# A hybrid decoder block on one core: attention heads spliced into the weight stream at other places, unnormalised differential weights, and the gate's modulation rows moved and given to VectorE alone

## The reference

```python
shift, scale, gate = split(c @ w_ada + b_ada, 3)
h = rms_norm(x, g_pre) * (1 + scale) + shift
proj = h @ w_in            # MLA q / kv latent / rope key, diff q / k / v, two SiLU gates, two merge gates
o_mla  = mla_attention(...)                  # 8 heads, softmax, causal
lam = exp(sum(lq1 * lk1)) - exp(sum(lq2 * lk2)) + lambda_init
a = p[:, 0] - lam * p[:, 1]                  # 8 differential heads, each with two softmax maps
o_diff = rms_norm(a @ v, g_subln) * (1 - lambda_init)
y_mla, y_diff = (o_mla * silu(gate_mla)) @ w_o_mla, (o_diff * silu(gate_diff)) @ w_o_diff
merged = sigmoid(mg_mla) * y_mla + sigmoid(mg_diff) * y_diff
x = x + gate * rms_norm(merged @ w_out, g_post)
```

## Time and profile before

| what | value |
|---|---|
| median of 3 runs | 806.49 us (806.04 to 807.21) |
| profiled execution, its own time | 807.88 us |
| its span | 806.1 us |
| PE busy | 763.9 us (95%) |
| DVE busy | 560.5 us (70%) |
| ACT busy | 399.4 us (50%) |
| POOL busy | 129.4 us (16%) |
| DMA | 190.23 MB, mean 236 GB/s |
| TensorE's granted clock, mean | 0.992 |

### The profile page before, as it was taken

One profiled execution on the slowest core, in us unless ns is written; L12 is line 12 of the kernel. 1 busy time (PEld: TensorE's weight loads), 2 busy tenths in 40 slices (PEclk: granted clock), 3 DMA queues, 4 the chain that ended last, 5 costly groups with the idle time before them and its releaser, 6 DMA issues.

```text
span 806.1 us, 9875 instructions
## 1 busy us (share of the span) xinstructions
PE 763.9 (95%) x3565; PEld 624.8 (77%) x3565; DVE 560.5 (70%) x795; ACT 399.4 (50%) x634; POOL 129.4 (16%) x149
## 2 busy tenths in 40 slices
PE   4789999999999999999999999989999999989995
PEld 4567888787888788888887777767888888868884
DVE  4888888798676845455546999888777766475553
ACT  4466646445665565444446464635344443343441
POOL 2000000000000000000004441454264254210000
PEclk9899999999999999999999999999999999999998
DMA  9999999999664465555456767666687778765542
GB/s 340 392 321 378 342 312 332 322 332 309 213 202 133 156 210 158 157 157 152 136 178 233 244 211 231 194 228 207 210 288 264 234 259 274 276 231 183 189 151 104
DMA packets 116795, 190.23 MB, mean 236 GB/s; under 512 B 9797, under 2 KB 42762, under 8 KB 116234
## 3 DMA queue, kind: packets, MB, share of 16 engines
q1 hardware_dynamic: 116624, 189.56, 71.5%
q10 hardware_dynamic: 122, 0.04, 0.0%
HBM read 187.47 MB, written 2.10 MB: 235 GB/s over the span
## 4 chain that ended last, share of the span: by engine, by line
PE 69%; DVE 14%; DMA 5%; issue 5%; ACT 4%; SPq 2%; POOL 1%; DVEq 0%; POOLq 0%; ACTq 0%
PE ps L1581 21%; PE ps L1585 21%; PE ps L1582 21%; DVE w_both L1328 5%; DVE ada_acc L1125 3%; DMA w_raw<-in_w_out 2%; DMA w_raw<-in_w_in 2%; SPq L416 1%; ACT w_both L884 1%; DMA ada_ring<-in_w_ada 1%; PE ps L1373 1%; PE ps L1417 1%; PE ps L1426 1%; PE ps L1430 1%; PE ps L1456 1%
## 5 line engine op out<-in xcount | busy, mean ns | idle before, releaser
L1328 DVE TENSOR_TENSOR w_both<-w_raw,w_both 128x1024 fp32r<-128x1024 f32 x248 | 303.6, 1233 | 149.6 <-ACT w_both L884 148.6
L884 ACT CAST w_both<-w_raw 128x1024 fp32r<-128x1024 f32 x248 | 258.8, 1051 | 283.7 <-PE ps L1585 204.9
L1581 PE MATMUL ps<-w_both,h_hi 128*128 128x512 f32 x704 | 284.4, 404 | 6.7 <-DVE w_both L1328 6.1
L1585 PE MATMUL ps<-w_both,h_lo 128*128 128x512 f32 x704 | 275.7, 392 | 0.3 <-DVE h_lo L1237 0.3
L1582 PE MATMUL ps<-w_both,h_hi 128*128 128x512 f32 x704 | 274.9, 390 | 0.0
L1581 PEld LDWEIGHTS ps<-w_both,h_hi 128*128 128x128 f32 x704 | 132.6, 188 | 40.3 <-issue 10.3
L1585 PEld LDWEIGHTS ps<-w_both,h_lo 128*128 128x128 f32 x704 | 132.4, 188 | 29.9 <-DVE h_lo L1237 1.0
L1582 PEld LDWEIGHTS ps<-w_both,h_hi 128*128 128x128 f32 x704 | 132.8, 189 | 26.3 <-issue 0.7
L1125 DVE SCALAR_TENSOR_TENSOR ada_acc<-ada_ring,cols,ada_acc 128x512 f32<-128x512 f32 x112 | 78.1, 743 | 1.7 <-DMA ada_ring<-in_w_ada 1.7
L534 POOL TENSOR_SCALAR gate_ring<-gate_ring,cols 128x512 f32<-128x512 f32 x28 | 50.0, 1787 | 65.9 <-DMA gate_ring<-in_w_ada 65.3
L1581 PE MATMUL ps<-w_both,o_hi 128*128 128x512 f32 x128 | 50.7, 396 | 0.0
(11 more groups left out here) (224 smaller groups left out, 728.0 us busy)
## 6 DMA issues: line engine op xcount, KB each, us to landing
w_raw<-in_w_in SPq DMA_DIRECT2D x177, 512.0 KB, 4.7
ada_ring<-in_w_ada SPq DMA_DIRECT2D x128, 256.0 KB, 6.5
gate_ring<-in_w_ada SPq DMA_DIRECT2D x32, 512.0 KB, 5.1
w_raw<-in_w_out SPq DMA_DIRECT2D x32, 512.0 KB, 3.7
w_raw<-in_w_o_mla SPq DMA_DIRECT2D x16, 512.0 KB, 4.4
w_raw<-in_w_o_diff SPq DMA_DIRECT2D x16, 512.0 KB, 5.7
w_raw<-in_w_ukv SPq DMA_DIRECT2D x8, 512.0 KB, 4.0
x_tok<-in_x SPq DMA_DIRECT2D x2, 1024.0 KB, 6.0
```

The source lines that it names most:

```text
L884: act.copy(w_hi[:, p % RING, :], w_raw[:, p % RING, :]).then_inc(hi_done, 1)
L1328: dve.tensor_tensor(w_lo[:, p % RING, :], w_raw[:, p % RING, :], w_hi[:, p % RING, :].bitcast(F32), ALU.subtract).then_inc(lo_done, 1)
L1581: mm(o, lhsT=s_hi[:, k, q], rhs=hi, start=first and r == 0, stop=False)
L1585: ins = mm(o, lhsT=s_lo[:, k, q], rhs=hi, start=False, stop=last and r == tiles - 1)
```

## The change

- Weights of a differential head: before, both maps were scaled with their own inverse sums and subtracted. Now the second map is multiplied by `ratio` = -lam * sum1 / sum2 and added to the first, which stays unnormalised. The missing factor 1 / sum1 (`first_scale`) is applied where the squares are made and, by one more GpSimd instruction, to the inverse root.
- `dve_o_lo` takes one instruction where it took two or three.
- Places: differential heads have t = s+5, v = s+7, g = s+10, MLA heads +4, +6, +8, so that TensorE's work for three neighbouring heads meets behind one piece, and there are two insertions per head. Before, there were three. `diff_weights` stands at s+7, `diff_out` still at v+5, which is now the same piece, behind the next head's weights.
- Gate: VectorE adds odd and even rows, GpSimd none. Part k stands at piece 173 + 2k (to 235); `gate_sum` is at 187, 204, 220, 236. `bias_gain` lies elsewhere and its first load waits for the differential heads.

The diff, without the declarations:

```diff
@@ -247,7 +249,7 @@
         ada_rings = [sb("ada_ring", [P, ADA_RING // 2, 2, 2, 2 * P], F32, r_c),
                      sb("ada_ring2", [P, ADA_RING // 2, 2, 2, 2 * P], F32, r_b)]
         silu_gate = sb("silu_gate", [P, 2, TOK, D // 2], F32, r_c)
-        bias_gain = sb("bias_gain", [P, 2, CH], F32, r_c + 4 * KB)
+        bias_gain = sb("bias_gain", [P, 2, CH], F32, r_c + 8 * KB)
         m_hi = sb("m_hi", [P, KT, SEQ], F32R, r_b)
         m_lo = sb("m_lo", [P, KT, SEQ], F32R, r_b + 16 * KB)
@@ -367,8 +368,8 @@
         MLA0 = last_piece("ukv", 0) + 6
         DIFF0 = first_piece("mm", 0) + 4
-        mla_at = [(MLA0 + 4 * h, MLA0 + 4 * h + 3, MLA0 + 4 * h + 5, MLA0 + 4 * h + 7) for h in range(HEADS)]
-        diff_at = [(DIFF0 + 5 * h, DIFF0 + 5 * h + 6, DIFF0 + 5 * h + 8, DIFF0 + 5 * h + 11) for h in range(HEADS)]
+        mla_at = [(MLA0 + 4 * h, MLA0 + 4 * h + 4, MLA0 + 4 * h + 6, MLA0 + 4 * h + 8) for h in range(HEADS)]
+        diff_at = [(DIFF0 + 5 * h, DIFF0 + 5 * h + 5, DIFF0 + 5 * h + 7, DIFF0 + 5 * h + 10) for h in range(HEADS)]
         G_QN, G_CKV, G_QR, G_KR, G_KN, G_D = 0, 4, 6, 8, 9, 13
@@ -396,7 +397,7 @@
         acc_of_group = lambda j: ada_acc if j % 2 == 0 else ada_acc2
         ada_slot = lambda n: ada_rings[n % ADA_RING // 4][:, n % 4, :, :, :]
-        GATE0, GATE_STEP = first_piece("mm", 0) + 5, 3
+        GATE0, GATE_STEP = first_piece("mm", 0) + 52, 2
         gate_parts_at = {GATE0 + GATE_STEP * k: (k,) for k in range(4 * (KT // 2))}
         gate_end = [GATE0 + GATE_STEP * (8 * n + 7) for n in range(4)]
         gate_sum_at = [gate_end[n] + (n > 0) for n in range(4)]
@@ -422,7 +423,6 @@
                 k = n * (KT // 2) + i
                 if k >= 2:
                     sp.wait_ge(gate_used, k - 1)
-                    sp.wait_ge(gate_used_pool, k - 1)
                 else:
                     sp.wait_ge(pv_done, HEADS)
                 col = 2 * D + n * CH
@@ -432,7 +432,7 @@
             def load_bias_gain(n):
                 if n == 0:
-                    sp.wait_ge(o_gated_ready, HEADS)
+                    sp.wait_ge(o_gated_ready, 2 * HEADS)
                 else:
                     sp.wait_ge(gg_ready, n)
                 sp.dma_start(bias_gain[:, 0, :], b_ada[0, 2 * D + n * CH:2 * D + (n + 1) * CH]
@@ -523,19 +523,6 @@
                                     fill=-NEG_INF / min(SLOPES), base=0, pattern=[[-1, P]],
                                     channel_multiplier=1).then_inc(consts, 1)
-            products = [0]
-            def add_odd_rows(ring, cc, fresh, used, count):
-                if fresh:
-                    nc.gpsimd.tensor_scalar(ada_acc[:, 1, :], ring, cc, None, ALU.mult).then_inc(used, 1)
-                else:
-                    products[0] += 1
-                    nc.gpsimd.tensor_scalar(ring, ring, cc, None, ALU.mult).then_inc(odd_products, 1)
-                    pool.wait_ge(odd_products, products[0])
-                    pool.wait_ge(used, count - 1)
-                    nc.gpsimd.tensor_tensor(ada_acc[:, 1, :], ada_acc[:, 1, :], ring, ALU.add).then_inc(used, 1)
             inverse_root(R_CKV, ckv_sq, 1, RANK)
             def head_root(h):
@@ -548,25 +535,13 @@
                 pool.wait_ge(var_ready, k)
                 nc.gpsimd.tensor_tensor(variance[:, k, :], variance[:, k, :], power[:, :], ALU.pow).then_inc(root_ready, 1)
                 pool.wait_ge(root_ready, h + 1)
-                nc.gpsimd.tensor_tensor(rstd[:, k, :], variance[:, k, :], in_range[:, :], ALU.mult).then_inc(rstd_ready, 1)
+                nc.gpsimd.tensor_tensor(rstd[:, k, :], variance[:, k, :], in_range[:, :], ALU.mult).then_inc(head_root_ready, 1)
+                pool.wait_ge(head_root_ready, h + 1)
+                nc.gpsimd.tensor_tensor(rstd[:, k, :], rstd[:, k, :], first_scale[:, h % 2, 1, :], ALU.mult).then_inc(rstd_ready, 1)
                 pool.wait_ge(rstd_ready, k)
-            def odd_gate_rows(k):
-                n, i = k // (KT // 2), k % (KT // 2)
-                pool.wait_ge(gate_in[k % 2], 16 * (k // 2 + 1))
-                if k == 0:
-                    pool.wait_ge(ada_turned, KT // 2)
-                if i == 0 and n >= 1:
-                    pool.wait_ge(gate_summed, n)
-                add_odd_rows(gate_ring[:, k % 2, CH:2 * CH], cols[:, V_C + 2 * i + 1:V_C + 2 * i + 2],
-                             i == 0, gate_used_pool, k + 1)
-            work = [(place, 0, lambda k=parts[0]: odd_gate_rows(k)) for place, parts in gate_parts_at.items()]
-            work += [(diff_at[h][2] + 4, 1, lambda h=h: head_root(h)) for h in range(HEADS)]
-            for place, _, run in sorted(work, key=lambda w: w[:2]):
-                run()
+            for h in range(HEADS):
+                head_root(h)
             for t in range(TOK):
                 pool.wait_ge(y_sums, t + 1)
                 nc.gpsimd.tensor_scalar(variance[:, R_Y, t:t + 1], sumsq[:, R_Y, t:t + 1], 1.0 / D, EPS,
@@ -1017,11 +992,12 @@
             def run(eng):
                 src = ps[:, 7, SEQ:2 * SEQ]
                 eng.wait_ge(o_hi_ready, m + 1)
-                if m >= HEADS:
-                    link(eng, dve.tensor_scalar(tmp[:, 0:SEQ], src, cols[:, NVEC:NVEC + 1], None, ALU.mult))
-                    src = tmp[:, 0:SEQ]
-                link(eng, dve.tensor_tensor(o_lo[:, m, :], src, o_hi[:, m, :].bitcast(F32), ALU.subtract))
-                dve.memset(gain_tmp[:, 0:1], 0.0).then_inc(o_lo_ready, 1)
+                if m < HEADS:
+                    ins = dve.tensor_tensor(o_lo[:, m, :], src, o_hi[:, m, :].bitcast(F32), ALU.subtract)
+                else:
+                    ins = dve.scalar_tensor_tensor(out=o_lo[:, m, :], in0=src, scalar=cols[:, NVEC:NVEC + 1],
+                                                   in1=o_hi[:, m, :].bitcast(F32), op0=ALU.mult, op1=ALU.subtract)
+                ins.then_inc(o_lo_ready, 1)
             return run
         def diff_scores(h):
@@ -1045,27 +1021,27 @@
             def run(eng):
                 eng.wait_ge(exps_done, m + 1)
                 link(eng, dve.reciprocal(recip[:, m % 2, :], sums[:, m % 2, :]))
-                second = recip[:, m % 2, :].rearrange("p (b w) -> p b w", w=2)[:, :, 1]
-                link(eng, dve.tensor_scalar(second, second, lam[:, 0:1], None, ALU.mult))
-                spans = ((0, P), (P, KEYS))
-                for b, (lo, hi) in enumerate(spans):
-                    ins = dve.tensor_scalar(probs[:, m % 2, 1, lo:hi], probs[:, m % 2, 1, lo:hi],
-                                            recip[:, m % 2, 2 * b + 1:2 * b + 2], None, ALU.mult)
+                by_map = lambda x, w: x[:, m % 2, :].rearrange("p (b w) -> p b w", w=2)[:, :, w]
+                dve.tensor_scalar(first_scale[:, m % 2, 0, :], by_map(recip, 0), SQ_SCALE, None, ALU.mult)
+                dve.tensor_copy(first_scale[:, m % 2, 1, :], by_map(recip, 0))
+                link(eng, dve.scalar_tensor_tensor(out=ratio[:, m % 2, :], in0=by_map(recip, 1), scalar=neg_lam[:, 0:1],
+                                                   in1=by_map(sums, 0), op0=ALU.mult, op1=ALU.mult))
+                for b, (lo, hi) in enumerate(((0, P), (P, KEYS))):
+                    ins = dve.scalar_tensor_tensor(
+                        out=probs[:, m % 2, 0, lo:hi], in0=probs[:, m % 2, 1, lo:hi], scalar=ratio[:, m % 2, b:b + 1],
+                        in1=probs[:, m % 2, 0, lo:hi], op0=ALU.mult, op1=ALU.add)
+                ins.then_inc(weights_ready, 1)
+            return run
+        def head_squares(h):
+            def run(eng):
+                eng.wait_ge(pv_done, HEADS + h + 1)
+                for t in range(TOK):
+                    ins = dve.tensor_scalar(tmp[:, t * P:(t + 1) * P], ps[:, 7, t * P:(t + 1) * P],
+                                            first_scale[:, h % 2, 0, t:t + 1], SQ_CLAMP, ALU.mult, ALU.min)
                 link(eng, ins)
-                for b, (lo, hi) in enumerate(spans):
-                    ins = dve.scalar_tensor_tensor(
-                        out=probs[:, m % 2, 0, lo:hi], in0=probs[:, m % 2, 0, lo:hi],
-                        scalar=recip[:, m % 2, 2 * b:2 * b + 1], in1=probs[:, m % 2, 1, lo:hi],
-                        op0=ALU.mult, op1=ALU.subtract)
-                ins.then_inc(weights_ready, 1)
-            return run
-        def head_squares(h):
-            def run(eng):
-                eng.wait_ge(pv_done, HEADS + h + 1)
-                link(eng, dve.tensor_scalar(tmp[:, 0:SEQ], ps[:, 7, 0:SEQ], SQ_SCALE, SQ_CLAMP, ALU.mult, ALU.min))
                 for t in range(TOK):
                     part = tmp[:, t * P:(t + 1) * P]
                     ins = dve.scalar_tensor_tensor(out=tmp[:, SEQ + t * P:SEQ + (t + 1) * P], in0=part, scalar=-SQ_CLAMP,
@@ -1134,15 +1110,15 @@
                     eng.wait_ge(gate_summed, n)
                 if k == 0:
                     eng.wait_ge(ada_turned, KT // 2)
```

(62 more changed lines are left out.)

## The result

The changed kernel takes 814.85 us (median of 5 runs, 814.33 to 816.78), the kernel before 807.21 us beside it. The ratio is 1.0104, with a 95% interval of 1.0087 to 1.012: some 8 us slower, where +1.6 us was forecast. The span of the profiled execution is 815.0 us against 806.1; it is the slowest of the five (816.78 us).

A forecast was written before the change was run, and what follows sets the result against it. TensorE was taken to set the end, so only its waits could move: heads -3.9, insertions 0, late gate places +0.9, +2.0 and +2.6, sum +1.6 us, median 808.1 us; range 804.0 to 812.0.

The forecast's parts named there:

- Insertions: TensorE's insertions fall from 66 to 47 places with the same instructions: 0 us, bounds -1 and +1.
- Heads: Differential heads: -7.6 us from gate work leaving, +3.7 from probs wanted one piece earlier; sum -3.9, bounds -6.5 and -1.5.
- (a): Pieces 205 and 221: a group's first gate part waits about 6.7 us for gate_sum; TensorE late at 208, +0.9 us.
- (b): Pieces 218 to 220: late gate loads push w_raw 217 and 218 into x_again's 2 MB: +2.0 us, bounds -0.5 and +3.
- (c): Before piece 223: m_lo late behind part 24, gate load 26 and w_raw 225; wait 4.2 us against 1.6, +2.6.
- the forecast's 0.165: Time added to each TensorE wait, since a matmul's bar of 0.39 us reaches 0.16 us past its turn of 0.23.
- Late waits: Gate work in pieces 173 to 235, with three dearer places near 208, 218 to 220 and 223: +5.5 us.
- rival 2: Before piece 223: the 4.2 us wait may drop the clock to 1.2 GHz, 1.7 us lost; +3.3, 809.8 us; chance 0.16.

The follow-up runs named there:

- heads_only: The changed kernel's head part alone (weights, o_lo, places), gate as in the kernel before, with one more wait putting gate_finish behind the squares: 808.01 us, ratio 1.0011.
- fill_half: The changed kernel with unread small matmuls (9, 8, 9 and 15) on TensorE ahead of four of its waits: 811.81 us, ratio 1.0059.
- experiment 4: The changed kernel with a second pair of accumulators for the gate's groups 1 and 3: 806.04 us, ratio 0.9993.
- experiment 6: The changed kernel with every gate part and sum one piece earlier: 812.16 us, ratio 1.006.
- experiment 7: Second load of x twelve pieces later in SyncE's queue: on the changed kernel 808.79 us, ratio 1.0031; on the kernel before 804.48 us, ratio 0.9973.

## Why the prediction was wrong

The steps in their order.

**Insertions: 0 was close.** From the insertion at 88 to that at 125, with 32 places before and 20 after, the time is 0.7 us less. It was within the bounds.

**Heads: right.** Said were waits at heads 0 and 5 of 2.7 and 1.0 us; the trace has 2.5 and 0.6, and none else. Weights were put at 1.45 us and took 1.41. The table load ends at 434.10+1.28 = 435.38, and the exponentials lie between that and the casts at 437.17, 1.8 us as before. That is the row's price; the 2.66 us of the Trainium skill (ScalarE: Activation LUTs, What ACT_TABLE_LOAD costs) do not show here.

**(a) Right in place, wrong in mechanism.** 208 waits 0.7 us (said: 0.9). VectorE's waits for gate_sum:

```profile
DVE ada_acc L1098 <- PE ps L1475: 9.6, 3, 4.0
```

They were to be 6.7 us at pieces 205 and 221, and are 4.0 at most. My reading, which no run tested by itself: VectorE came later to them, since it had lost its lead, and what costs is less how long it stands than that it starts again with no lead.

**(b) and (c): right in kind, too small in (b).** Waits of 0.8 and 2.7 us were said at 218 and 220; they are 2.2 and 2.4 (here and below a row's wait plus the forecast's 0.165). For m_lo 4.2 was said, it is 4.1. (The terms of (b) add up to 3.5-1.7 = 1.8, where the sum has 2.0; that changes nothing.) But no wait at 213 and 214 stands in the forecast, and they wait 0.7 us each. SyncE, ScalarE, VectorE and TensorE from 680 us on:

```profile
680.12 0.37 SPq L429 DMA_DIRECT2D gate_ring<-in_w_ada  x1
680.53 0.47 SPq L438 DMA_DIRECT2D bias_gain<-in_b_ada  x1
681.04 0.43 SPq L440 DMA_DIRECT2D bias_gain<-in_g_post  x1
681.52 0.96 SPq L449 DMA_DIRECT2D w_raw<-in_w_o_diff  x2
...
689.09 1.05 ACT L859 CAST w_both<-w_raw 128x1024 fp32r<-128x1024 f32 x1 [6.31 <-DMA w_raw<-in_w_o_diff]
...
721.77 0.88 DVE L1098 TENSOR_SCALAR ada_acc<-gate_ring,cols 128x512 f32<-128x512 f32 x2 [3.95 <-PE ps L1475]
...
722.68 0.37 SPq L429 DMA_DIRECT2D gate_ring<-in_w_ada  x1
723.10 1.09 SPq L449 DMA_DIRECT2D w_raw<-in_w_out  x2
...
728.40 1.04 ACT L859 CAST w_both<-w_raw 128x1024 fp32r<-128x1024 f32 x1 [5.18 <-DMA w_raw<-in_w_out]
...
730.69 1.22 DVE L1090 TENSOR_TENSOR m_lo<-ps,m_hi 128x1024 fp32r<-128x1024 f32 x1
...
731.96 0.80 PE L1562 MATMUL ps<-w_both,m_hi 128*128 128x512 f32 x1 [3.89 <-DVE m_lo L1090]
```

SyncE was held by a gate part, then issued gate part 20, both bias_gain rows and pieces 213 and 214 in 2.4 us. Issue to landing of the four pieces issued from 681.5 to 686 us:

```profile
DMA to landing us min/median/max: 7.5/8.2/8.3
```

The forecast has some 5 us from issue to landing, the median of the earlier trace rows, and leaves bias_gain out. By that piece 213 would have come at about 686.5; it came at 689.1. What part the bias_gain rows have in this no run shows. The burst at 218 began later too: x_again went out at 694.8, 4 us behind the end of piece 212, where the forecast had it at about that end. The end of the list is as forecast: first gate part of the last group at 721.77, gate load 26 and piece 225 issued at 722.7 and 723.1, cast at 728.40, m_lo at 730.69, piece 223 at 731.96.

Late waits, with the 0.165 us for each, are then 9.8+6 x 0.165 = 10.8 us against 3.2: +7.6 where +5.5 was forecast. Heads: 2.8+0.3 = 3.1 against 7.6: -4.5 where -3.9 was forecast. With the insertions -0.7 that would have been +2.4 us. That this is near the +1.6 is in part luck: the late waits were put 2.1 us too low, heads and insertions 1.3 us too high.

**The step that failed: rival 2, the clock.** It was priced at 1.7 us, at one place, with a chance of 0.16, and kept out of the sum. The trace shows it at three places: the span grew by 8.9 us, of which the terms above explain 2.4. The argument against it was that before a wait of 2.7 us had brought no fall. The wait behind piece 130 did. Twelve us around it in the changed kernel, and in the run with second accumulators, which has the same wait:

```profile
436.00:448.00 12.00, 9.62 (x35) 6.90 (x34) 6.83 (x13) 4.57 (x10) 0.00 (x0) 0.72 0.42 132
```

```profile
434.00:446.00 12.00, 9.62 (x48) 7.38 (x47) 7.61 (x14) 6.42 (x14) 0.00 (x0) 1.00 0.46 143
```

TensorE is busy for 9.62 us in both, but makes 35 matmuls in one and 48 in the other, at a clock of 0.72 and of 1.00. Thus the same wait brings a fall in some executions and none in others: of six profiled executions with it, three fell (in one of them, heads_only, behind an earlier wait and fall). That one row of no fall proves nothing is what the forecast missed. And at the place that rival 2 named, before piece 223, it was no matter of chance: all nine profiled executions with a wait of 2.0 to 3.9 us there fell, and none with 1.5 us or less. The rule of the Trainium skill (TensorE: Matmul & The Clock Gate, HAM oscillation) that waits for transfers re-throttle the clock was borne out there, and should have had most of the chance. Its example has waits of some 3 to 5 us; here waits of 2.0 to 2.5 us did it too, and those were for VectorE.

What a fall costs can be read from the traces. From the last matmul of piece 130 (438.01 in the changed kernel, above) to the first of piece 136, with the same work and the same wait between; below them in the run with second accumulators, then two neighbours at half speed:

```profile
461.11 0.50 PE L1562 MATMUL ps<-w_both,h_hi 128*128 128x512 f32 x1
```

```profile
436.82 0.39 PE L1571 MATMUL ps<-w_both,o_lo 128*128 128x512 f32 x1
...
456.90 0.50 PE L1567 MATMUL ps<-w_both,h_hi 128*128 128x512 f32 x1
```

```profile
718.24 0.63 PE L1562 MATMUL ps<-w_both,m_hi 128*128 128x512 f32 x1
718.67 0.63 PE L1563 MATMUL ps<-w_both,m_hi 128*128 128x512 f32 x1
```

That is 23.1 us against 20.1: 3.0 us for the stretch of 6.8. A turn at half speed is 0.43 us where it is 0.23; 8 such turns from 717.0 on make 1.6 us, 13 from 731.96 on 2.6. Together 7.2, where 6.5 were left over; the 0.7 between them isn't settled. Not all of it need reach the end: with the falls gone others wait longer, and fill_half won back 3.0 us. So the clock's part of the loss lies between these 3 and 7 us. The median lies lower than this execution: with mean clocks of 0.982 to 0.984 against 0.980 the other four ran an estimated 3 to 7 us less at half speed ((1 - clock) x 2 x 815 us).

What the chain hangs on is shown by experiment 4: VectorE's wait for gate_sum, removed, gives back 8.8 us. Starting the gate's list a piece earlier gives 2.7 us (experiment 6), and taking the 2 MB of x out of the burst gives 6 (experiment 7).

## What to carry to other kernels

When TensorE is at 95%, price each new wait of 2 us or more twice: its length, and what a stretch at half speed may cost behind it (here 1.6 us for 3.4 us, 3.0 for 6.8). When work is packed denser behind a stage, look first for waits in the engine's own list that are written for the old spacing (here: accumulators free one piece after the sum in place of two), and give them a second buffer. Price transfers in a burst by rows from a burst (here 7.5 to 8.3 us), and not by the median of all loads (5.1 us); a load that isn't wanted until the end goes away from the burst.

## What the runs showed of the hardware

A fall of the clock isn't a function of the wait alone: the same wait of 2.5 us behind piece 130 left TensorE at 2.4 GHz in three profiled executions and took it to 1.2 GHz in three. The wait before piece 223 took it there in all nine in which it was 2.0 us or longer. The stretches at half speed lasted 3.4 or 6.8 us and cost 1.6 and 3.0 us where TensorE had work throughout (from the end of piece 130 to piece 136: 20.1 us without a fall, 21.7 with one of 3.4, 23.1 with one of 6.8). A small float32 matmul of 128 columns stands in the trace as two records and takes 0.23 us among its like (30 of them 6.9 us), double what the spacing of single records had suggested.
